# Scaling the first branch's exponentials on GpSimd instead of ScalarE in a two-layer hybrid attention block

## The reference

```python
def attend(q, k, v, scale, mask=None, sink=None):
    s = einsum('bqhgd,bkhd->bhgqk', q, k) * scale
    p = softmax(s, axis=-1)            # exp(s - max) / sum(exp(s - max))
    return einsum('bhgqk,bkhd->bqhgd', p, v)
```

## Time and profile before

| | |
|---|---|
| median of three runs | 1783.62 us (1778.84 to 1785.39) |
| profiled execution: its span, first to last instruction | 1785.1 us |
| PE busy | 1711.1 us (96%) |
| DVE busy | 1084.0 us (61%) |
| ACT busy | 1049.3 us (59%) |
| POOL busy | 528.0 us (30%) |
| mean granted clock of TensorE | 0.980 |

### The profile page before, as it was taken

The page is one execution under the profiler, slowest core; times in us unless marked ns, Lnnn a source line. Parts: engine busy times, 40 slices in busy tenths (PEclk is TensorE's granted clock), DMA queues, the critical chain, the costliest instruction groups (busy, mean ns, idle before and its releaser), DMA issues.

```text
span 1785.1 us, 27001 instructions
## 1 busy us (share of the span) xinstructions
PE 1711.1 (96%) x10554; PEld 1498.7 (84%) x10554; DVE 1084.0 (61%) x2185; ACT 1049.3 (59%) x1921; POOL 528.0 (30%) x300
## 2 busy tenths in 40 slices
PE   7999999999999999999999999999999999999997
PEld 3777888889989889899889996788888887888787
DVE  5543776765565566665775655477775756565634
ACT  3433778766666777666321253577776677786322
POOL 1523123222232212212322353322333432332442
PEclk9997999999999999999999999899999999999999
DMA  9111102111121111111644331111212221212642
GB/s 326 40 37 28 26 24 55 27 42 48 42 60 43 47 37 36 42 48 36 201 153 166 118 97 49 40 34 37 60 48 66 72 64 44 60 49 65 200 142 95
DMA packets 178527, 129.53 MB, mean 73 GB/s; under 512 B 21661, under 2 KB 167647, under 8 KB 178400
## 3 DMA queue, kind: packets, MB, share of 16 engines
q1 hardware_dynamic: 174242, 115.37, 22.7%
q10 hardware_dynamic: 2878, 8.24, 1.3%
q0 software_dynamic: 1280, 4.20, 0.7%
HBM read 123.58 MB, written 4.19 MB: 72 GB/s over the span
## 4 chain that ended last, share of the span: by engine, by line
PE 76%; DVE 10%; ACT 7%; issue 3%; POOL 2%; DMA 1%; SPq 0%; DVEq 0%; ACTq 0%; POOLq 0%
PE acc L1357 56%; PE wide L1415 6%; PE ptp L1435 6%; PE pv L1448 4%; PE pv L1449 3%; DVE nmax L1991 2%; ACT e L1682 2%; DVE pt L2016 1%; DMA w_raw<-in_ada_w 1%; POOL h_lo L1844 1%; DVE k_m L1552 1%; ACT w_hi L1600 1%; DVE k_s L1552 1%; DVE q_s L1552 1%; POOL w_lo L1806 1%
## 5 line engine op out<-in xcount | busy, mean ns | idle before, releaser
L1806 POOL TENSOR_TENSOR w_lo<-w_raw,w_hi 128x1024 fp32r<-128x1024 f32 (+2 forms) x192 | 392.0, 2045 | 1085.0 <-ACT w_hi L1600 1084.8
L1357 PE MATMUL acc<-h_hi,w_hi 128*128 128x512 f32 (+2 forms) x1320 | 463.3, 352 | 10.3 <-DVE cq_lo L1554 3.9
L1357 PE MATMUL acc<-h_hi,w_lo 128*128 128x512 f32 (+2 forms) x1320 | 462.0, 351 | 0.0
L1357 PE MATMUL acc<-h_lo,w_hi 128*128 128x512 f32 (+2 forms) x1320 | 457.7, 350 | 0.3 <-POOL h_lo L1844 0.3
L1991 DVE TENSOR_REDUCE nmax<-wide 128x1 f32<-128x768 f32 (+3 forms) x240 | 189.6, 790 | 167.9 <-PE wide L1415 166.2
L1357 PEld LDWEIGHTS acc<-h_hi,w_hi 128*128 128x128 f32 (+1 forms) x1320 | 248.4, 188 | 50.1 <-issue 7.9
L1697 ACT ACTIVATE pt<-ptp 128x512 fp32r<-128x512 f32 (+3 forms) x312 | 165.8, 563 | 210.4 <-PE ptp L1435 208.6
L1357 PEld LDWEIGHTS acc<-h_hi,w_lo 128*128 128x128 f32 (+1 forms) x1320 | 248.2, 188 | 33.4
L1357 PEld LDWEIGHTS acc<-h_lo,w_hi 128*128 128x128 f32 (+1 forms) x1320 | 246.1, 188 | 34.2 <-POOL h_lo L1844 0.5
L1689 ACT ACTIVATE e<-e,einv 128x768 f32<-128x768 f32 (+3 forms) x240 | 193.5, 806 | 70.2 <-DVE einv L2008 69.8
L2016 DVE TENSOR_TENSOR pt<-ptp,pt 128x512 fp32r<-128x512 f32 (+3 forms) x312 | 191.8, 640 | 43.9 <-ACT pt L1697 43.7
(11 more groups left out here) (216 smaller groups left out, 3103.1 us busy)
## 6 DMA issues: line engine op xcount, KB each, us to landing
w_raw<-in_w_in SPq DMA_DIRECT2D x102, 512.0 KB, 3.9
w_raw<-in_ada_w SPq DMA_DIRECT2D x48, 512.0 KB, 5.3
w_raw<-in_w_out SPq DMA_DIRECT2D x16, 512.0 KB, 4.2
w_raw<-in_w_in SPq DMA_DIRECT2D x16, 256.0 KB, 3.3
w_raw<-in_w_o_mla SPq DMA_DIRECT2D x16, 256.0 KB, 2.8
w_raw<-in_w_o_swa SPq DMA_DIRECT2D x16, 256.0 KB, 2.8
w_raw<-in_w_o_ax SPq DMA_DIRECT2D x16, 256.0 KB, 2.9
w_raw<-in_mla_w_uq SPq DMA_DIRECT2D x16, 144.0 KB, 2.4
```

The costliest lines, as they stand in the source:

```text
L1357: ins = nc.tensor.matmul(dst, lhs, rhs, start=first, stop=last)
L1806: nc.gpsimd.tensor_tensor(w_lo[s][:, 0:k], w_raw[s][:, 0:k], f(w_hi[s][:, 0:k]), ALU.subtract).then_inc(w_lo_ready, 1)
```

## The change

The first branch (`mla`) is scaled on GpSimd, with `tensor_scalar` by `einv`; `swa` and `ax` stay on ScalarE. TensorE's transposes wait for the semaphore of the engine that scaled. VectorE now also waits, before it writes `einv` in column n modulo 8, until GpSimd has read that column for unit n-8. VectorE's instructions stay the same, since its own scaling code was never reached.

```diff
-        on_act, invs, norms = BRANCHES, {}, {}
+        on_pool, by_act, by_pool = BRANCHES[:1], {}, {}
...
-                    if u["branch"] in on_act:
-                        if new(norm_act, invs[u["n"]]):
-                            pe.wait_ge(norm_act, invs[u["n"]])
-                    elif new(norm_done, norms[u["n"]]):
-                        pe.wait_ge(norm_done, norms[u["n"]])
+                    if u["branch"] in on_pool:
+                        if new(norm_pool, by_pool[u["n"]]):
+                            pe.wait_ge(norm_pool, by_pool[u["n"]])
+                    elif new(norm_act, by_act[u["n"]]):
+                        pe.wait_ge(norm_act, by_act[u["n"]])
...
-                elif ev == "N" and e["u"]["branch"] in on_act:
+                elif ev == "N" and e["u"]["branch"] not in on_pool:
...
+                elif ev == "N" and e["u"]["branch"] in on_pool:
+                    u = e["u"]
+                    if new(inv_done, u["n"] + 1):
+                        pool.wait_ge(inv_done, u["n"] + 1)
+                    r = u["n"] % 8
+                    nc.gpsimd.tensor_scalar(e_of(u), e_of(u), einv[:, r:r + 1], None, ALU.mult).then_inc(norm_pool, 1)
...
-                    if u["branch"] in on_act:
-                        nc.vector.reciprocal(einv[:, r:r + 1], total[:, r:r + 1]).then_inc(inv_done, 1)
-                        continue
-                    link(nc.vector.reciprocal(einv[:, r:r + 1], total[:, r:r + 1]))
-                    nc.vector.tensor_scalar(e_of(u), e_of(u), einv[:, r:r + 1], None, ALU.mult).then_inc(norm_done, 1)
+                    if u["n"] - 8 in by_pool:
+                        if new(norm_pool, by_pool[u["n"] - 8]):
+                            dve.wait_ge(norm_pool, by_pool[u["n"] - 8])
+                    nc.vector.reciprocal(einv[:, r:r + 1], total[:, r:r + 1]).then_inc(inv_done, 1)
```

More of the change, by code:

```diff
@@ L1037, in build @@
         stat_done, th_done = semaphore("stat_done"), semaphore("th_done")
-        s_done, max_done, exp_done, norm_done = (semaphore(k) for k in ("s_done", "max_done", "exp_done", "norm_done"))
-        inv_done, norm_act = semaphore("inv_done"), semaphore("norm_act")
+        s_done, max_done, exp_done = (semaphore(k) for k in ("s_done", "max_done", "exp_done"))
+        inv_done, norm_act, norm_pool = semaphore("inv_done"), semaphore("norm_act"), semaphore("norm_pool")
         pt_done, pt_hi_ready, pt_lo_ready = semaphore("pt_done"), semaphore("pt_hi_ready"), semaphore("pt_lo_ready")
@@ L1171, in _ @@
                     sp.wait_ge(out_saved[i], 16 * (TT - TT_CTX) // 2)
-        on_act, invs, norms = BRANCHES, {}, {}
+        on_pool, by_act, by_pool = BRANCHES[:1], {}, {}
         for e_ in events:
             if e_["ev"] == "N":
-                counts = invs if e_["u"]["branch"] in on_act else norms
+                counts = by_pool if e_["u"]["branch"] in on_pool else by_act
                 counts[e_["u"]["n"]] = len(counts) + 1
@@ L1683, in _ @@
                                          bias=nbias[:, r:r + 1], scale=scale, accum_out=esum[:, r:r + 1]).then_inc(exp_done, 1)
-                elif ev == "N" and e["u"]["branch"] in on_act:
+                elif ev == "N" and e["u"]["branch"] not in on_pool:
                     u = e["u"]
-                    if new(inv_done, invs[u["n"]]):
-                        act.wait_ge(inv_done, invs[u["n"]])
+                    if new(inv_done, u["n"] + 1):
+                        act.wait_ge(inv_done, u["n"] + 1)
                     r = u["n"] % 8
```

## The result

The changed kernel takes 1827.04 us, the median of four runs (1824.76 to 1831.65), against 1783.38 us before on the same chip (1778.84 to 1785.39). The ratio is 1.0247, with a 95% interval of 1.0223 to 1.0271. Predicted were 1790.5 us in 1777 to 1811. The profiled execution's span is 1825.0 us against 1785.1, 39.9 us more.

What follows compares the result with a forecast made beforehand. PE was taken to bound the kernel. Late transposes 9.6 + VectorE 1.5 + clock 1 - ScalarE's relief 5 = +7.1 us on the profiled 1785.1; set against the median, 1790.5 us, range 1777 to 1811.

Steps and rivals of the forecast that it cites:

- The bound: Whole run: PE, busy 96%, sets the time; its idle time in the mla windows, 21 us, caps any gain.
- The duration: GpSimd's scaling of 768 columns takes 1.15 us, between 0.75 and 1.84 us, since the second input is what goes.
- The place in the queue: mla scalings behind ropes and w_lo on POOL make 16 of 40 passes' transposes late: 13.8 us, 9.6 after deductions.
- the working: Pass-by-pass layout of scalings behind POOL's earlier work in the old trace, compared with transpose starts: 13.8 us late.
- the prediction's signs: Expected in the profile after: some ten PE waits for POOL's e, 8 to 12 us, longest just behind rope pairs.
- The deduction at 324.70: Transposes 2.2 us late behind a rope there cost nothing, falling into PE's existing 2.48 us wait at 330.85.
- ScalarE's relief: Taking 67.9 us of mla scaling off ACT shortens PE's waits by 5 us, bounds 0 and 16.
- VectorE beside POOL: Some dozen two-input VectorE instructions in mla windows lose 6 us beside scalings; 1.5 us reaches PE, bounds 0 and 6.
- The clock: PE's new waits of 1.7 to 2 us seldom lower its clock: 1 us, bounds 0 and 7.
- Rival 1: POOL's one-input scaling costs 1.84 us like two-input ones; transposes late in 21 passes, +25 us, 1809; chance 0.20.

Runs made afterwards that it cites:

- relief: The changed kernel with the mla scaling left out on every engine, transposes waiting for the inverse alone (output not the reference's): 1784.75 us, ratio 0.9995.
- first: The changed kernel with only the first unit of each mla pass scaled on GpSimd, the second on ScalarE as before: 1791.11 us, ratio 1.0038.
- warm: The changed kernel with 142 unused matmuls ahead of TensorE's wait for GpSimd's scaling in 17 passes: 1817.19 us, ratio 1.0207.
- tt: The changed kernel with GpSimd's scaling as tensor_tensor with einv broadcast over the columns, same queue place: 1809.36 us, ratio 1.0151.

## Why the prediction was wrong

1. *The bound.* Right. PE's waits decide; the engines' busy shares told nothing of the sign.
2. *The duration, 1.15 us, bounds 0.75 to 1.84.* This is the step that failed. It is 2.226 us, above the upper bound. "The second input is what goes" took the missing input for the price. The runs show that the form of the instruction sets it: at the same shape copy 0.82, broadcast product 1.49, `tensor_scalar` 2.14 with a constant and 2.21 with a column. An upper bound from the nearest row of the same engine was no bound, because that row was another instruction. The figure of the Trainium skill's "GPSIMD Engine Reference" (1.8 cycles an element, an estimate of 1.15 us) was as far off.
3. *The place in the queue.* Right in kind and passes. All 16 passes in which PE waited for GpSimd are among the 28 that the working marks as late at 2.22 us, and 14 of the 16 are late at 1.15 us already. The long ones stand at ropes and `w_lo`: 3.93 us where 1.69 was worked out for 1.15 us, 3.23 for 2.23. But the two longest (3.93 and 3.36 us) are behind a `w_lo`, not behind a rope as the prediction's signs had it. With the measured duration this term is 39.4 us by the working, 30.3 by the trace, where 9.6 was put.
4. *The deduction at 324.70*, 2.2 us to be absorbed by the wait at 330.85: that older wait is gone after the change, as said.
5. *ScalarE's relief, 5 us.* It is 0 within 0.3% (`relief`). The waits of the earlier trace rows together fell only from 18.5 to 16.9 us, and the time of an execution not measurably. ScalarE's part of them, 1.7 us, did not go: PE waits 1.9 us for the exponentials instead.
6. *VectorE beside POOL, 1.5 us.* The size on VectorE was about right: in the two stretches 12 of its `q_m` and `o_t` are stretched by over a quarter, where 5 were before, 13.2 us in place of 4.7 (6 us more were expected). Five of the 12 start inside a scaling, others beside a `w_lo` or a rope whose moment had shifted. PE's waits for VectorE's low parts grew from 4.5 to 8.2 us in the second stretch and fell from 4.8 to 1.8 in the first. In `first`, where the lock-out stands nearly alone, it goes with some 6 us.
7. *The clock, 1 us, at most 7.* Mis-sized too: 12.6 us at least (`warm`), 17.3 by PE's busy time. PE waited nine times for more than 2 us for a scaling (2.15 to 3.93), and beside eight of these stands a stay of 3.4 to 6.8 us at 1.2 GHz; the exception is one of 2.78 us, soon after another stay. The premise was wrong as well. From one wait of 2.96 us with a fall and one of 2.48 without, the prediction concluded that waits of 1.7 to 2 us lie below both. In `tt` stays start within a microsecond of the start of the transposes that had waited 1.57, 1.81 and 1.97 us, and the kernel before has one itself, behind a wait of 1.17 us. PE's instruction, then the window with the clock of 0.57 (columns as in the earlier trace rows):

```profile
200.18 0.49 PE L1448 MATMUL pv<-pt,v_m 128*128 128x256 f32 x1 [1.17 <-DVE o_half L2023]
...
200.00:204.00 4.00, 3.82 (x16) 3.56 (x17) 3.02 (x8) 3.66 (x7) 2.24 (x1) 0.57 0.03 6
```

With the copy, near the duration that the forecast assumed, the lower clock takes 10.2 us, 6.8 more than before: some 3 us of time.

The forecast's 9.6 + 1.5 + 1 - 5 = 7.1 us were in truth, in the two stretches, 27.7 us of idle time (late transposes with what was lost and won on VectorE) + 17.3 (clock) - 0 (relief) = 45.0 us. This split is of one difference and proves nothing by adding up; the runs that change one term at a time do. Rival 1 was the right one, at a price beyond its own: it named 25 us from 1.84 us a scaling. Its turning point, "slower than 0.5% from about 1.25 us on", is between the 0.82 us (1.0047) and the 1.49 us (1.0151) of the curve. Left open is how much of the 45 us is the lock-out, and how many of `first`'s 6.5 us; no kernel without it was tried.

## What to carry to other kernels

Before work moves to GpSimd, look for the very instruction (operation, operands, type) in a trace; a row of a neighbour is no bound, here 2.2 us against 0.8, 1.5 and 1.8 us for the same columns. Then lay it behind what already stands in that engine's queue and compare with the moment at which the reader wants it: a table made so from the trace of before names the late passes one by one, and its sum is right to some 15% while the lateness is small (30% too high at 2.2 us). And ask first what the relief is worth: an engine that is 75% busy can lose 68 us and give nothing, if the next wait belongs to a neighbour. Short waits count twice: here PE's idle time of 28 us brought some 14 to 17 us of slower matmuls with it.

## What the runs showed of the hardware that was not expected

- GpSimd, 128 x 768 float32 in place: `tensor_copy` 0.82 us, `tensor_tensor` with a broadcast column 1.49, `tensor_scalar` with a constant 2.14, with a column 2.21; for 256 columns 0.45, 0.61, 0.85 and 0.92 us.
- VectorE's `tensor_scalar` on the same rows took 0.62 us for 768 columns and 0.35 us for 256 where GpSimd ran nothing beside it, but 2.61 us at most and 1.00 and 0.85 us in the mean. It has only one full input in SBUF and a column; still, every long one started while a GpSimd instruction was running.
- TensorE's lower clock appears behind short waits too: stays of 3.4 us at 1.2 GHz stand at waits of 1.17 us (before), 1.57 and 1.81 us (`tt`), but not at one of 2.48 us.
- Filling TensorE's waits with unused matmuls won 4 to 10 us of 1827, by the clock alone.
